# State-space decay weights: the causal mask added by the matrix engine, the decay rows sent twice, and the step size taken into the exponent

## The reference, cut to what matters

```python
def step(h, inp):
    x_i, dt_i, b_i, c_i = inp
    acs = jnp.cumsum(dt_i * A, axis=1)
    seg = jnp.where(tril, acs[:, :, None] - acs[:, None, :], -jnp.inf)
    wts = jnp.einsum('btgn,bsgn->btsg', c_i, b_i)[..., None] * jnp.exp(seg) * dt_i[:, None]
    y = (jnp.einsum('btsgr,bsgrp->btgrp', wts, x_i)
         + jnp.einsum('btgn,bgrpn->btgrp', c_i, h) * jnp.exp(acs)[..., None])
    to_end = jnp.exp(acs[:, -1:] - acs) * dt_i
    h = (h * jnp.exp(acs[:, -1])[..., None, None]
         + jnp.einsum('bsgn,bsgr,bsgrp->bgrpn', b_i, to_end, x_i))
    return h, y
```

## Time and profile before

| | |
|---|---|
| time, median of 3 runs | 3853.36 us (3842.98, 3853.36, 3854.19) |
| profiled execution, its own time | 3847.22 us |
| its span (first to last instruction) | 3845.3 us |
| PE busy | 3546.2 us (92%) |
| DVE busy | 1830.4 us (48%) |
| ACT busy | 979.2 us (25%) |
| the groups of the state-space part | 1592 to 2035 us of the span |

### The profile page before, as it was taken

The page is one execution under the profiler, slowest core; times in us unless marked ns, Lnnn a source line. Parts: engine busy times, 40 slices in busy tenths (PEclk is TensorE's granted clock), DMA queues, the critical chain, the costliest instruction groups (busy, mean ns, idle before and its releaser), DMA issues.

```text
span 3845.3 us, 55014 instructions
## 1 busy us (share of the span) xinstructions
PE 3546.2 (92%) x23444; PEld 2310.2 (60%) x23444; DVE 1830.4 (48%) x3030; ACT 979.2 (25%) x1881; POOL 410.9 (11%) x937
## 2 busy tenths in 40 slices
PE   7988998989999998999989988888888999999999
PEld 5788878866444445777767762222345433577887
DVE  4575367650122123688885430110246467745443
ACT  4422252331111113456654130000024200221000
POOL 1133013310000000000000000000040058200000
PEclk8998999999999998999999989999998999999999
DMA  5332333234989984122002429999921012231331
GB/s 214 108 95 59 121 115 88 71 132 171 384 337 356 358 338 160 56 78 88 34 34 66 131 89 417 420 421 421 375 73 56 22 50 66 77 122 59 110 110 55
DMA packets 305987, 628.41 MB, mean 163 GB/s; under 512 B 74064, under 2 KB 242512, under 8 KB 246864
## 3 DMA queue, kind: packets, MB, share of 16 engines
q1 hardware_dynamic: 303120, 624.25, 44.2%
q10 hardware_dynamic: 2624, 0.66, 0.1%
HBM read 608.60 MB, written 16.25 MB: 162 GB/s over the span
## 4 chain that ended last, share of the span: by engine, by line
PE 55%; DVE 10%; DMA 9%; ACT 3%; issue 2%; DVEq 0%; ACTq 0%
PE ps L1783 12%; PE ps L2065 11%; PE ps L1789 4%; DMA arena<-moe_w_down 4%; PE ps L2128 4%; DMA arena<-moe_w_up 2%; PE ps L2305 2%; DMA arena<-moe_w_gate 2%; PE ps L1353 2%; PE ps L1358 2%; PE ps L1349 2%; ACT arena L2804 2%; PE ps L1873 1%; DVE arena L3833 1%; PE ps L2365 1%
## 5 line engine op out<-in xcount | busy, mean ns | idle before, releaser
L1783 PE MATMUL ps<-arena 128*64 128x512 f32 x3072 | 706.1, 599 | 74.5 <-DMA arena<-moe_w_down 24.1
L1783 PEld LDWEIGHTS ps<-arena 128*64 128x64 f32 x3072 | 205.8, 136 | 523.0 <-issue 375.7
L1349 PE MATMUL ps<-h_second,w_rest 128*128 128x512 f32 (+1 forms) x1088 | 363.7, 351 | 1.8 <-DVE h_second L3122 1.5
L3546 DVE SCALAR_TENSOR_TENSOR arena<-arena,ps 128x512 f32<-128x512 f32 (+1 forms) x48 | 30.2, 657 | 555.3 <-PE ps L1783 555.3
L1349 PEld LDWEIGHTS ps<-h_second,w_rest 128*128 128x128 f32 x1088 | 208.5, 192 | 30.1 <-DVE h_second L3122 3.7
L1353 PE MATMUL ps<-h_first,w_rest 128*128 128x512 f32 (+1 forms) x576 | 208.5, 377 | 0.6 <-DVE arena L3707 0.5
L2735 ACT ACTIVATE m_yx_lead<-ps 64x512 fp32r<-64x512 f32 x64 | 37.9, 592 | 613.3 <-PE ps L1783 612.6
L3833 DVE TENSOR_TENSOR arena<-arena,ps 128x512 f32<-128x512 f32 x86 | 58.4, 687 | 269.6 <-ACT arena L3037 141.1
L3554 DVE TENSOR_TENSOR m_yx_rest<-ps,m_yx_lead 64x512 fp32r<-64x512 f32 x64 | 44.1, 689 | 297.1 <-ACT m_yx_lead L2735 296.0
L1789 PE MATMUL ps<-arena 128*32 128x256 f32 x3072 | 175.7, 380 | 0.0
L2128 PE MATMUL ps<-arena 128*128 128x512 f32 x384 | 168.5, 594 | 0.7 <-ACT arena L2959 0.7
(11 more groups left out here) (576 smaller groups left out, 7151.0 us busy)
## 6 DMA issues: line engine op xcount, KB each, us to landing
arena<-moe_w_gate SPq DMA_DIRECT2D x128, 1024.0 KB, 9.1
arena<-moe_w_up SPq DMA_DIRECT2D x128, 1024.0 KB, 9.7
arena<-moe_w_down SPq DMA_DIRECT2D x128, 1024.0 KB, 11.9
arena<-ada_w SPq DMA_DIRECT2D x48, 1024.0 KB, 6.8
arena<-ffn_w_gate_up SPq DMA_DIRECT2D x22, 1024.0 KB, 5.1
arena<-gdn_w_in SPq DMA_DIRECT2D x16, 1024.0 KB, 9.4
arena<-w_in SPq DMA_DIRECT2D x28, 512.0 KB, 4.0
arena<-ssd_w_x SPq DMA_DIRECT2D x8, 1024.0 KB, 4.8
```

The costliest lines, as they stand in the source:

```text
L1349: rests = lambda k: pe.matmul(out, wh[:, k, cols_], hT_lo[k][:, x], start=False, stop=(tail_from is not None and k == KD - 1))
L1783: mm = pe.matmul(ps[CAPX * h:CAPX * h + CAPX, bank, :], x[:, 0:CAPX], w[:, 512 * h:512 * h + 512], **flags)
```

## The change

Four things are changed, in all 32 output steps.

1. The mask is added by PE. `ssd_scores` first multiplies the mask (copied four times side by side into a new tile `masks_r`) by an identity matrix into bank `2*d`, and the decay rows are accumulated on top of it.
2. ACT takes exp of the masked rows directly out of PSUM into `s_D`, for both directions, ahead of the plain exp.
3. PE then sends the plain rows again into the same bank (new function `ssd_rows`), since `s_Ce` needs them without the mask. In the program of PE this stands between the 16 leading and the 8 remaining matmuls of the fill (the new argument `inside`). ACT takes their exp into `s_Ce` after that.
4. dt is no longer multiplied into the tokens; ln(dt) is added once to the bias `s_a` in `ssd_scalars` (one more logarithm on ACT, with its table load), and the outputs read the plain tokens.

DVE thus loses lines 3684 and 3686 in every output step; it multiplies `s_D` by C.B first, then weighs tokens for the state, and multiplies `s_Ce` by C last. The preparation of the next rows waits for the second sending.

```diff
@@ ahead of the groups
+        ident_r = rounded_tiles("s_one_lead", 1, ARENA + 2 * P, P)[0][:, :]
+        masks_r = rounded_tiles("s_masks", 1, ARENA + 3 * P, 2 * SR * P)[0][:, :]
...
@@ PE: split_product, and ssd_tile, which hands inside on
+                if inside:
+                    inside()
                 pe.wait_ge(*rest_of_chunk(item))
...
@@ PE: ssd_scores
-                    pe.matmul(ps[:, 2 * d, :], side_sel[:, d * P:(d + 1) * P], s_spot, start=True, stop=True)
+                    pe.matmul(ps[:, 2 * d, :], ident_r, masks_r[:, d * SR * P:(d + 1) * SR * P], start=True, stop=False)
+                    pe.matmul(ps[:, 2 * d, :], side_sel[:, d * P:(d + 1) * P], s_spot, start=False, stop=True)
                     mm = pe.matmul(ps[:, 2 * d + 1, 0:P], s_B[g % 2][:, cx], s_C[:, cx], start=True, stop=True)
                     mm.then_inc(s.r_in, 1)
+
+            def ssd_rows(g, st):
+
+                nx = 4 * g + st - 2
+                for d in range(2):
+                    pe.wait_ge(s.r_d, R_IN + 2 * nx + d + 1)
+                    pe.matmul(ps[:, 2 * d, :], side_sel[:, d * P:(d + 1) * P], s_spot, start=True, stop=True).then_inc(s.r_dm, 1)
@@ PE: ssd_outputs
-                            pe.matmul(out(r), s_xdt[d][:, r, :], s_D[d][:, r, :], start=True, stop=False)
+                            pe.matmul(out(r), s_xtok[g % 2][:, CHUNK_OF[d][st], r * SP_:(r + 1) * SP_], s_D[d][:, r, :], start=True, stop=False)
@@ PE: ssd_groups
-                    fill(0, 1)
+                    fill(0, 1, lambda: ssd_rows(g, 2))
...
-                        fill(st - 2, 0)
+                        fill(st - 2, 0, lambda: ssd_rows(g, st))
@@ ACT: ssd_scalars
+                a.do(act.activation(s_lndt, s_lndt, ACT.Ln), s.tl_act)
@@ ACT: ssd_decays
                 for d in range(2):
-                    act.wait_ge(s.r_dm, R_IN + 2 * nx + d + 1)
+                    act.wait_ge(s.r_in, R_IN + 2 * nx + d + 1)
                     if nx:
                         act.wait_ge(s.s_y, 2 * (nx - 1) + d + 1)
-                    a.do(act.activation(s_Ce[d].rearrange("p a b -> p (a b)"), ps[:, 2 * d, :], ACT.Exp), s.r_eb)
                     for r in range(SR):
                         h = 32 * d + SR * g + r
-                        x = s_D[d][:, r, :]
-                        a.do(act.activation(x, x, ACT.Exp, bias=s_a[:, CHUNK_OF[d][st], h:h + 1]), s.r_d if r == SR - 1 else None)
+                        a.do(act.activation(s_D[d][:, r, :], ps[:, 2 * d, r * P:(r + 1) * P], ACT.Exp, bias=s_a[:, CHUNK_OF[d][st], h:h + 1]),
+                             s.r_d if r == SR - 1 else None)
+                for d in range(2):
+                    act.wait_ge(s.r_dm, R_IN + 2 * nx + d + 1)
+                    a.do(act.activation(s_Ce[d].rearrange("p a b -> p (a b)"), ps[:, 2 * d, :], ACT.Exp), s.r_eb)
@@ DVE: ssd_scalars
+                v.do(dve.tensor_scalar(s_lndt, s_dt, 1e-18, None, ALU.max))
...
+                v.do(dve.tensor_copy(ident_r, ident))
+                for d in range(2):
+                    v.do(dve.tensor_copy(masks_r[:, d * SR * P:(d + 1) * SR * P].rearrange("p (r i) -> p r i", r=SR), negm[:, d, :].unsqueeze(1).to_broadcast([P, SR, P])))
...
+                dve.wait_ge(s.tl_act, 6)
+                v.do(dve.tensor_tensor(s_a, s_a, s_lndt, ALU.add))
@@ DVE: ssd_spread
-                        dve.wait_ge(s.r_in, R_IN + 2 * nx)
+                        dve.wait_ge(s.r_dm, R_IN + 2 * nx)
@@ DVE: ssd_step
                 if st >= 2:
                     for d in range(2):
-                        v.do(dve.tensor_tensor(s_xdt[d], xt[d], over(s_dt[:, tile[d], hs[d]]), ALU.mult))
-                        dve.wait_ge(s.r_in, R_IN + 2 * nx + d + 1)
-                        v.do(dve.tensor_tensor(s_D[d], ps[:, 2 * d, :].rearrange("p (r i) -> p r i", i=P),
-                                               negm[:, d, :].unsqueeze(1).to_broadcast([P, SR, P]), ALU.add), s.r_dm)
+                        dve.wait_ge(s.r_d, R_IN + 2 * nx + d + 1)
+                        v.do(dve.tensor_tensor(s_D[d], s_D[d], ps[:, 2 * d + 1, 0:P].unsqueeze(1).to_broadcast([P, SR, P]), ALU.mult))
+                if st < 5:
+                    for d in range(2):
+                        v.do(dve.tensor_tensor(s_xe[d], xt[d], over(s_te[:, tile[d], hs[d]]), ALU.mult), s.s_xend)
+                if st >= 2:
                     for d in range(2):
                         cx = slice((tile[d] - XT0) * P, (tile[d] - XT0 + 1) * P)
                         dve.wait_ge(s.r_eb, R_IN + 2 * nx + d + 1)
-                        v.do(dve.tensor_tensor(s_Ce[d], s_Ce[d], s_C[:, cx].unsqueeze(1).to_broadcast([P, SR, P]), ALU.mult))
-                        dve.wait_ge(s.r_d, R_IN + 2 * nx + d + 1)
-                        v.do(dve.tensor_tensor(s_D[d], s_D[d], ps[:, 2 * d + 1, 0:P].unsqueeze(1).to_broadcast([P, SR, P]), ALU.mult), s.r_w)
+                        v.do(dve.tensor_tensor(s_Ce[d], s_Ce[d], s_C[:, cx].unsqueeze(1).to_broadcast([P, SR, P]), ALU.mult), s.r_w)
                     ssd_spread(nx + 1)
```

More of the change, by code:

```diff
@@ L704, in build @@
         side_sel = rounded_tiles("s_side_rows", 1, ARENA, 2 * P)[0][:, :]
+        ident_r = rounded_tiles("s_one_lead", 1, ARENA + 2 * P, P)[0][:, :]
+        masks_r = rounded_tiles("s_masks", 1, ARENA + 3 * P, 2 * SR * P)[0][:, :]
+        s_lndt = plain_tile("s_ln_dt", ARENA + (3 + 2 * SR) * P, NT * 2 * SH).rearrange("p (t h) -> p t h", t=NT)
         s_D = [carve(SR, P) for _ in range(2)]
@@ L708, in build @@
         so_hi = rounded_tiles("so_lead", 1, top[0] + -top[0] % 8) + rounded_tiles("so_lead_h", 3, base)
-        s_xdt = [carve(SR, SP_) for _ in range(2)]
         s_xe = [carve(SR, SP_) for _ in range(2)]
@@ L1343, in _, with split_product @@
             gdn_tail()
-            def split_product(out, item, w, cols_, x, high, tail_from=None):
+            def split_product(out, item, w, cols_, x, high, tail_from=None, inside=None):
                 wh, wl = w
@@ L1927, in ssd_scalars, with ssd_tile @@
                 mm.then_inc(s.tl_spread, 1)
-            def ssd_tile(g, i, part):
+            def ssd_tile(g, i, part, inside=None):
                 item = (("sx", g), ("sx", g), ("sbc", g), ("sbc", g))[i]
@@ L1951, in ssd_tile @@
                     mm = split_product(ps[:, 4 + 2 * (i % 2) + part, 0:nn], item, state.w, slice(m * P, (m + 1) * P), slice(c0, c0 + nn),
-                                       hT_hi, (lambda k: KD + 2 * k + 2, lambda k: KD + k + 1) if g == i == part == 0 else None)
+                                       hT_hi, (lambda k: KD + 2 * k + 2, lambda k: KD + k + 1) if g == i == part == 0 else None, inside)
                     if part == (1 if i < 3 else 0):
@@ L2021, in ssd_groups, with fill @@
                 for g in range(SG):
-                    def fill(i, part):
+                    def fill(i, part, inside=None):
                         if g + 1 < SG:
-                            ssd_tile(g + 1, i, part)
+                            ssd_tile(g + 1, i, part, inside)
+                        elif inside:
+                            inside()
                     fill(0, 0)
@@ L3690, in ssd_step @@
                         dve.wait_ge(s.r_eb, R_IN + 2 * nx + d + 1)
-                        v.do(dve.tensor_tensor(s_Ce[d], s_Ce[d], s_C[:, cx].unsqueeze(1).to_broadcast([P, SR, P]), ALU.mult))
-                        dve.wait_ge(s.r_d, R_IN + 2 * nx + d + 1)
-                        v.do(dve.tensor_tensor(s_D[d], s_D[d], ps[:, 2 * d + 1, 0:P].unsqueeze(1).to_broadcast([P, SR, P]), ALU.mult), s.r_w)
-                if st >= 2:
+                        v.do(dve.tensor_tensor(s_Ce[d], s_Ce[d], s_C[:, cx].unsqueeze(1).to_broadcast([P, SR, P]), ALU.mult), s.r_w)
                     ssd_spread(nx + 1)
-                if st < 5:
-                    for d in range(2):
-                        v.do(dve.tensor_tensor(s_xe[d], xt[d], over(s_te[:, tile[d], hs[d]]), ALU.mult), s.s_xend)
                 if st >= 3 and g + 1 < SG:
```

## The result

The changed kernel takes 3860.7 us (median of 15 runs, 3854.2 to 3869.5), the kernel before, in 15 runs beside it, 3849.7 us (3842.8 to 3854.3). The ratio is 1.0033, 95% interval 1.0024 to 1.0041. In a second set of runs it was 1.0021 (1.0012 to 1.0029). Forecast were 3860 us and a range of 3846 to 3876. The sum of +10.5 us stands against +11.0 and +8.0 in the medians of the two sets, and +7.0 between the two profiled executions (spans 3852.3 and 3845.3 us; the one of the changed kernel, 3854.18 us by its own time, is the shortest of its 15).

A forecast was written before the change was run, and what follows sets the result against it. PE was taken as the bound of filled groups (busy 54.09 of 57.90 us). Five groups +8.5 us, two +3.0 and the last -1 made +10.5: 3857.7 from the profiled execution, forecast as 3860, range 3846 to 3876.

The forecast's parts named there:

- Only PE counts: Groups with fill: work taken from DVE returns at most PE's 3.8 us idle and restarts; work added to PE counts nearly fully.
- A matmul of 0.24 us: Each output step: four added 128x512 matmuls at 0.24 us each cost 0.97 us, 31 us in 32 steps.
- rival C: Masks and second rows fall mostly into PE restarts already counted as busy: +3 us, 3852; chance 0.18.
- announced sign: Whole program: PE's busy time up by some 30 us would show the forecast right.
- Steps 3 and 4: Filled group: PE becomes the bound; step 3 gains 0.27 us (13.47), step 4 loses 0.5 us (13.27).
- Step 2: Filled group: wait on DVE exchanged for PE's own outputs, loss 0.4 us; about 0.2 without conditioning products.
- Step 5: Filled group: multiplication by C, now last, starts the convolution 1.07 us later, silu and tokens with it; loss 1.07 us.
- rival A: Second sending stalls PE in steps 4 and 5; 21 filled steps lose another 0.4 us: +8, about 3868; chance 0.18.
- Ahead of the groups: Before the groups: mask copies, logarithm and its table load are covered by waits, cost zero; 1.8 us without that cover.
- The last group: Group without fill: a chain through PE, DVE and ACT sets the pace, with PE's clock deciding; 1 us less taken.
- clock held and clock lost: Last group: 2.4 GHz held gives 9.0 us a step, 3.4 us less; 1.2 GHz throughout gives 12, 7 more.
- Rival B: Second sending finished by 3.9 us, step 5's convolution 0.7 us earlier, last group gives 10 us: 3839; chance 0.07.

The follow-up runs named there:

- dt alone: The kernel before with only the dt part of the change (dt in the exponent, DVE no longer weighs tokens by dt): 3847.5 us, ratio 0.9997.
- rows four later: The changed kernel with the second sending of the rows behind four of the last eight matmuls of the fill: 3872.1 us, ratio 1.0063 to before.
- dt back: The changed kernel without its dt part, DVE weighing tokens by dt again: 3859.3 us, ratio 1.0026 to before.

## Why the prediction was right, step by step

**Only PE counts (right).** DVE lost 7.3 us a group and the group grew by 1.3. What the relief by dt is worth can be read from dt alone: 0.45 us a group in the kernel before, nothing in the changed one. The larger part of the relief, the two mask additions a step, was not taken away by itself.

**A matmul of 0.24 us (right).** Doubling the masks measures 0.225 (0.45 us in steps 4 and 5). The rival C is out with it. What C pointed to is nevertheless real, and the sum had it: in scores that are waited for, one of the two masks hides in the gap of 0.44 us. That gap counts as busy before, and so PE's busy time is the one announced sign that failed: +30 us were forecast, +16.5 came. The scores of a group with fill, up to the start of the fill, took 4.57 us in group 1 before and 5.54 after, 0.97 for eight masks instead of 1.8; the sum had this, the sign had not.

**Steps 3 and 4 (right, 0.15 us too long each).** 13.47 and 13.27 us were forecast, 13.32 and 13.10 measured. The lead of 1.30 at unwaited scores is 1.29 (1675.78 to 1677.07). The term that was off is the 16 leading matmuls: I had read 3.87 us in step 4 of before, and here they take 3.73. The same trace of before had the shorter figure one step later, from 1687.26 to

```profile
1691.00 2.02 PE L1358 MATMUL ps<-h_first,w_rest 128*128 128x512 f32 x8
```

which is 3.74. Matmuls stand 0.236 us apart in one and 0.228 in the other, with no waits in either. In the kernel before, the slow pace comes in some of the steps 3 and 4, in the changed one only in some of the steps 3 (3.87 in groups 2, 5 and 6, where the step lasts 13.46, the forecast to 0.01). Those are the steps whose scores PE waits for, but with the rows four later it also came in three steps without such a wait. Its cause is open. The granted clock is 1.00 in all of them, and transfers don't decide it: step 4 of group 0 before has 3.74 us at a DMA share of 0.60.

**Step 2 (right).** 9.17 forecast, 9.24 measured, with the wait at the next scores still for DVE, which now waits 0.46 and 0.45 us for PE's outputs, as told. In the two groups without conditioning products step 2 is 8.77 and 8.78, as before (8.78 and 8.77); 0.2 of loss was forecast there.

**Step 5 (right in kind, 0.2 us too much).** The second sending goes out 5.03 us after the scores (5.17 forecast, the same 0.14), the convolution begins at 7.91 (8.1), the tokens come at 11.93 (12.14), and the step is 0.85 longer instead of 1.07. Moving the second rows moves this step, as the theory wants. The last link was wrong: I had the tokens and silu carry the delay into the next group. It is DVE's work without a gap up to the head. The amount is the same, but an order that only brings silu earlier brings nothing.

**ACT and rival A (A wrong).** Eight exps out of PSUM take 2.18 us, where two times four out of SBUF took 2.54, which was the price taken. The groups of ACT by form, first of the changed kernel, then of before (busy us, mean ns of one):

```profile
L2817 ACT ACTIVATE arena<-ps,arena 128x128 f32<-128x128 f32 x256 | 69.7, 385 | 50.2 <-PE ps L1989 50.1
```

```profile
L2804 ACT ACTIVATE arena<-arena 128x128 f32<-128x128 f32 x256 | 81.3, 393 | 0.0
```

One exp is only 8 ns shorter, but the next starts sooner: 0.256 us from start to start (2.18 less one length, over seven) against 0.292 (1.27 less one length, over three), 36 ns less. The 272 ns of busy time for one (69.7 us over 256) lie under the lower bound of 283 that I had from the earlier trace rows. The Trainium skill ("VectorE: DVE Perf Modes", the section on the TRN2 errata) gives ScalarE a fixed cost 52 cycles at 1.2 GHz smaller from PSUM, which is 43 ns: the spacing comes near it, the length doesn't. ACT is done 0.46 us ahead of PE in step 5, and PE never waits at a second sending in groups 0 to 6. In the last group, where no fill stands between, it waits there 0.43 to 0.54 us for ACT in each direction. Two matmuls earlier the margin in step 5 is gone.

**Ahead of the groups (right).** The logarithm's table load runs beside DVE's and PE's work. DVE's wait there is 9.13 instead of 10.17 us, and ACT still waits for PE behind it (ACT's timeline; the earlier trace rows is the row of before):

```profile
1558.79 1.28 ACT L2777 ACT_TABLE_LOAD   x1
...
1566.10 0.60 ACT L2789 ACTIVATE arena<-ps 128x512 f32<-128x512 f32 x1 [2.44 <-PE ps L1362]
```

**The last group (right only in the mean).** -1 was forecast. From its first scores to the fill behind its outputs it took 38.48 us before, 37.01 in the first trace after and 39.59 in the second. PE's outputs in steps 2 to 4, beside the earlier trace rows, in the first:

```profile
2012.02 0.44 PE L2007 MATMUL ps<-arena 128*64 128x128 f32 x4 [1.50 <-DVE arena L3716]
...
2022.11 0.44 PE L2007 MATMUL ps<-arena 128*64 128x128 f32 x4 [1.50 <-DVE arena L3716]
...
2030.90 0.70 PE L2007 MATMUL ps<-arena 128*64 128x128 f32 x4 [1.49 <-DVE arena L3716]
```

and in the second, the first two of them:

```profile
2012.08 0.51 PE L2007 MATMUL ps<-arena 128*64 128x128 f32 x4 [1.50 <-DVE arena L3716]
...
2022.48 0.66 PE L2007 MATMUL ps<-arena 128*64 128x128 f32 x4 [1.50 <-DVE arena L3716]
```

The idle stretch is 1.50 us in both, as forecast, but it settles nothing: the second outputs run at full speed (0.44) in one and not (0.66) in the other, and the steps are 10.07, 8.78 and 11.03 us against 10.38, 10.44 and 10.37. My two cases, clock held and clock lost, occur in the same program. The held one is sized right (9.0 forecast, 8.78 at a granted 1.00). The lost one was 12 us with the clock low throughout, and no trace has that: the granted clock was 0.84 in the steps of 10.38 and 10.44 us and 0.70 in the one of 11.03. The forecast of -1 was a mean of two cases, and that it lies between -1.5 and +1.1 is no proof of either.

**The sum.** Five groups grew by 6.75 us (8.5 forecast), the next two by 2.0 (3.0), and the last by -1.5 or +1.1. The 2.0 are made of -0.1 in group 5, where the trace of before had a fall of the clock (granted 0.97, step 5 at 23.93 us) and that of after had none, and +2.1 in group 6, where it was the other way round (0.94). Without these falls each would have grown by some 1.1 us, an estimate from the 1.24 us by which step 5 of groups 4 and 5 is longer where the clock fell, and from group 6 of the kernel with dt back, which kept its clock and took 55.36 us against 54.35 before. The rest of the program is the same length to a microsecond. The groups' share of +8.8 us is less than forecast, and the medians of the runs are +11 and +8. The forecast is right within what these can tell; that 3860 meets 3860.7 so closely is luck, since the sum was too large for the groups, and the first set of runs came out that much above the traces. Rival B needed a second sending finished by 3.9 us; it is finished at 5.5, and the convolution began 0.87 us later, not 0.7 earlier. B would not have come true with an earlier sending either: with none at all, the convolution begins 0.04 us earlier than before, not 0.7. (In the recorded chances 0.24 and 0.18 make 0.42, not 0.41; nothing hangs on it.)

## What to carry to other kernels

Before work is moved from a half idle engine to the full one, read in each step which of them ends last: relief is worth only what the full engine waits for the other, here 0.45 us a group for dt, while each added matmul costs its 0.23 us in nearly every step. When a round trip through other engines is cut into an in-order stream, its place is a cost of its own: put it as early as its producer allows (here two matmuls earlier, worth 0.44 us a group, 3 us of some 8), and follow what stands behind it on the engine that receives it. An order within a run of work without gaps changes who is served first, not when the run ends.

## What the hardware showed unexpectedly

- The same program kept PE's full clock through one step of the last group in one execution (8.78 us) and in no step in the other (10.37 to 10.44), with the same idle stretches of 1.50 us ahead. With dt back, a granted clock of 0.57 over 4 us also came at step 2 of a filled group and cost 1.5 us. The same was seen in two other kernels, once and three times; the other groups of the same executions, with the same waits there, show none.
- Matmuls of 128x512 without a wait stood 0.228 us apart in one step and 0.236 in another of the same group, at a granted clock of 1.00 in both and with no wait in either. Transfers don't decide it.
